# Intra-chunk attention levels of an HGRN2 layer on TensorE: 64-wide instead of 32-wide blocks, and two visits a turn instead of three

## What is computed

```python
def step(S, inp):
    qc, kc, vc, lc = inp
    b = jnp.cumsum(lc, axis=2)
    o = jnp.einsum('bhtd,bhde->bhte', qc * jnp.exp(b), S)
    diff = b[:, :, :, None, :] - b[:, :, None, :, :]
    decay = jnp.where(causal, jnp.exp(jnp.where(causal, diff, 0.0)), 0.0)
    a = jnp.einsum('bhtd,bhsd,bhtsd->bhts', qc, kc, decay)
    o = o + jnp.einsum('bhts,bhse->bhte', a, vc)
    ...
```

## Time and profile before

| what | value |
| --- | --- |
| median of 3 runs | 975.35 us (973.83 to 975.71) |
| the profiled execution: its own time | 975.35 us |
| its span | 973.5 us |
| TensorE busy | 953.5 us, 98% |
| VectorE, ScalarE, GpSimd busy | 620.1, 398.8, 395.4 us |
| mean granted clock of TensorE | 0.994 of full |

### The profile page before, as it was taken

The page is one execution under the profiler, slowest core; times in us unless marked ns, Lnnn a source line. Parts: engine busy times, 40 slices in busy tenths (PEclk is TensorE's granted clock), DMA queues, the critical chain, the costliest instruction groups (busy, mean ns, idle before and its releaser), DMA issues.

```text
span 973.5 us, 23670 instructions
## 1 busy us (share of the span) xinstructions
PE 953.5 (98%) x9958; PEld 902.2 (93%) x9958; DVE 620.1 (64%) x1223; ACT 398.8 (41%) x794; POOL 395.4 (41%) x295
## 2 busy tenths in 40 slices
PE   6999999999999999999999999999999999999996
PEld 6999999999999999899999999999998788788896
DVE  6467667667676766738932226467667867877635
ACT  7522324242424234325432233432227757865423
POOL 2265445454545444512244441442105534445343
PEclk9999999999999999999999999999999989999999
DMA  9521222313131313333233323321113223333104
GB/s 364 185 67 54 83 70 67 91 45 113 46 91 45 91 46 113 110 113 100 81 131 131 131 87 114 88 88 44 44 45 94 68 65 94 98 102 84 37 30 145
DMA packets 52921, 89.96 MB, mean 92 GB/s; under 512 B 15720, under 2 KB 34760, under 8 KB 52688
## 3 DMA queue, kind: packets, MB, share of 16 engines
q1 hardware_dynamic: 52528, 88.10, 28.2%
q10 hardware_dynamic: 288, 0.35, 0.1%
HBM read 70.80 MB, written 17.64 MB: 91 GB/s over the span
## 4 chain that ended last, share of the span: by engine, by line
PE 95%; DVE 2%; ACT 1%; issue 1%; DMA 0%; SPq 0%; DVEq 0%; ACTq 0%
PE G L1732 67%; PE G L2039 8%; PE R L1801 3%; PE R L1732 2%; PE R L1970 2%; PE R L1984 2%; PE R L1823 1%; PE R L1812 1%; PE R L1826 1%; PE R L2014 1%; PE R L2004 1%; PE R L1763 1%; PE R L1776 1%; DVE SP L1570 0%; PE R L1832 0%
## 5 line engine op out<-in xcount | busy, mean ns | idle before, releaser
L1732 PE MATMUL G<-XH,WH 128*128 128x344 f32 x1160 | 375.4, 326 | 7.5 <-ACT XH L963 7.5
L1732 PE MATMUL G<-XL,WH 128*128 128x344 f32 x1160 | 370.7, 322 | 1.5 <-DVE XL L1350 0.8
L1732 PE MATMUL G<-XH,WL 128*128 128x344 f32 x744 | 235.5, 320 | 0.0
L1732 PEld LDWEIGHTS G<-XH,WH 128*128 128x128 f32 x1160 | 218.7, 189 | 14.9 <-issue 12.3
L1732 PEld LDWEIGHTS G<-XL,WH 128*128 128x128 f32 x1160 | 218.3, 189 | 4.6 <-issue 3.2
L711 POOL TENSOR_TENSOR WL<-WR,WH 128x1024 fp32r<-128x1024 f32 x40 | 103.0, 2574 | 183.2 <-ACT WH L864 183.2
L1732 PEld LDWEIGHTS G<-XH,WL 128*128 128x128 f32 x744 | 139.7, 188 | 0.0
L1732 PE MATMUL G<-XL,WL 128*128 128x344 f32 x416 | 133.4, 321 | 0.0
L797 POOL TENSOR_TENSOR SP<-SP,small 128x1024 f32<-128x1024 f32 (+1 forms) x32 | 57.2, 1789 | 116.1 <-DVE small L1581 116.1
L745 POOL TENSOR_TENSOR K<-K,FP 128x512 f32<-128x512 f32 x48 | 66.6, 1388 | 73.7 <-PE R L1801 52.5
L864 ACT ACTIVATE WH<-WR 128x1024 fp32r<-128x1024 f32 x58 | 61.2, 1055 | 78.5 <-PE G L1732 52.6
(11 more groups left out here) (279 smaller groups left out, 1747.5 us busy)
## 6 DMA issues: line engine op xcount, KB each, us to landing
WR<-w SPq DMA_DIRECT2D x58, 512.0 KB, 3.9
A<-x SPq DMA_DIRECT2D x8, 516.0 KB, 7.2
FG<-head_scales SPq DMA_DIRECT2D x8, 516.0 KB, 3.6
RESO<-x SPq DMA_DIRECT2D x8, 516.0 KB, 4.5
h_spill<-H SPq DMA_DIRECT2D x8, 516.0 KB, 3.0
gate_spill<-EV SPq DMA_DIRECT2D x24, 172.0 KB, 2.1
RES<-h_spill SPq DMA_DIRECT2D x24, 172.0 KB, 2.5
SS<-states SPq DMA_DIRECT2D x8, 512.0 KB, 5.9
```

Of the source, the lines that this page charges most:

```text
L1732: return nc.tensor.matmul(U[unit_bank(NU * n + i)][:, 0:TU], w[:, n % 3, k, :], x[:, seg(i)], start=(k == 0 and p == 0), stop=(k == KT - 1 ...
```

## The change

For heads 0 to 6, levels 1 to 3 are done in slot 2, and levels 4 to 6 in slot 5; before, level 1 and half of level 2 in slot 2, the rest of 2 and level 3 in slot 4, levels 4 to 6 in slot 6. The transposes of the values move from slot 4 to slot 5, behind the levels, and their copies with them. VectorE's updates 3, 4 and 5 move from slot 4 to 2 (in front of the masked copies of levels 1 to 3), update 6 from 6 to 5. GpSimd's updates 3, 4 and 5 move from slot 4 to the start of slot 3, ahead of `prepare`; update 6 from 6 to 5; `decode_parts` from 3 to 4. ScalarE's copies of keys for levels 4 and 5 move from slot 5 to the start of slot 3, ahead of `prepare` and of the gates. For all eight heads the piece of levels 1 to 4 is 64 tokens wide instead of 32.

```diff
-    return {2: ((1, 0, NC), (2, 0, NC // 2)), 4: ((2, NC // 2, NC), (3, 0, NC)), 6: ((4, 0, NC), (5, 0, NC), (6, 0, NC))}
+    return {2: ((1, 0, NC), (2, 0, NC), (3, 0, NC)), 5: ((4, 0, NC), (5, 0, NC), (6, 0, NC))}
 def turned_values(r):
-    return 2 if r == HEADS - 1 else 4
+    return 2 if r == HEADS - 1 else 5
...
             for slot in range(9):
+                if slot == 3 and 0 <= r < HEADS - 1:
+                    for l in (3, 4, 5):
+                        update_k(r, l)
                 if slot % 3 == 0:
                     prepare(3 * it + slot // 3 + 2)
...
-                if slot == 3:
+                if slot == 4:
                     decode_parts(r)
-                for l in {0: (0, 1, 2), 4: (3, 4, 5), 6: (6,)}.get(slot, ()):
+                for l in {0: (0, 1, 2), 5: (6,)}.get(slot, ()):
                     update_k(r, l)
...
+                if slot == 3 and r >= 0:
+                    for l in copied_levels(r)[2:4]:
+                        copy_keys(r, l)
                 if slot % 3 == 0 and (it or slot):
                     prepare(3 * it + slot // 3 + 2)
...
-                if slot == 5 and r >= 0:
-                    for l in copied_levels(r)[2:4]:
-                        copy_keys(r, l)
...
-                    if r < HEADS - 1 and slot == 4:
+                    if r < HEADS - 1 and slot == 2:
                         for l in (3, 4, 5):
                             update_q(r, l)
-                    if r < HEADS - 1 and slot == 6:
+                    if r < HEADS - 1 and slot == 5:
                         update_q(r, 6)
...
-            w = max(32, 2 * h)
+            w = max(64, 2 * h)
```

## The result

The changed kernel takes 983.12 us (median of 6 runs, 981.6 to 984.54), beside 975.34 us for the kernel before (6 runs): a ratio of 1.0081, with a 95% interval of 1.0065 to 1.0097. It is slower, by 7.8 us; that is less than one per cent, but the interval is clear of 1. The profiled execution took 984.04 us, 0.9 us above the median, for a span of 982.0 us, 8.5 us longer than the span before; the mean granted clock is 0.994 in both.

A forecast was written before the change was run, and what follows sets the result against it. TensorE, busy 98% of the span, was taken to bound the kernel by the sum of its steps. Seven heads' +6.6 us and head 7's +1.4 make +8.0 on 975.35: 983.4 us, range 980 to 988.

The forecast's parts named there:

- step 1: Matmuls of levels 1 to 4, heads 0 to 6: rounds last as long as their weight loads, net +1.20 us a head.
- the load's own slope: Lower bound for levels 1 to 4: rounds cost 0.83 ns a column, mean 47 ns, -2.7 us, 980.7 us.
- step 2: TensorE's seams around the level visits, heads 0 to 6: 1.35 us before, 1.09 after, net -0.26 us a head.
- Per head: Heads 0 to 6 on TensorE: matmuls and seams together +0.94 us each, +6.6 us for seven heads.
- step 3: Head 7's four levels: matmuls from 2.14 to 3.30 us, seams from 0.28 to 0.55, together +1.4 us.
- The others and their cover: VectorE, GpSimd, ScalarE and SP: moved work comes later but stays covered; VectorE's 7.4 us piece has 6.6 us cover.
- all at nothing: Other engines' moved and delayed work, including weight loads, was priced at no added time.
- rival (c): New stall from VectorE's 7.4 us piece or later copies: 1 us a head gives 990 us; chance 0.07.
- The sum: Whole kernel: 6.6 + 1.4 = +8.0 us on 975.35 us, giving 983.4 us.

The follow-up runs named there:

- run 3: Changed kernel with levels 1 to 4 loading only 34 weight columns, same number of matmuls in two column tiles: 973.97 us, ratio 0.9986.
- run 4: Changed kernel with only 16 of 32 moving columns in each matmul of levels 1 to 4, weights unchanged: 983.04 us, ratio 1.0085.
- Run 1: Kernel before with pieces of levels 1 to 4 widened to 64 tokens, its three visits kept: 985.53 us, ratio 1.0111.
- run 2: Changed kernel with pieces of 32 tokens again, so only the two merged visits are left of the change: 980.58 us, ratio 1.006.
- run 8: Kernel with two visits and 32-token pieces, plus some 170 satisfied waits a turn between unit matmuls in slots 4 and 7: 1037.08 us, ratio 1.0632.
- run 7: Kernel with two visits and 32-token pieces, plus 32 small matmuls (128 instructions) at the program's start: 985.09 us, ratio 1.0109.
- run 9: Changed kernel with only level 3 of heads 0 to 6 in 64-token pieces, levels 1, 2 and 4 and head 7 at 32: 980.03 us, ratio 1.0039.
- run 10: Changed kernel with 32-token pieces in head 7 and level 4, and head 4's last-turn scaling moved behind the chunk states: 979.76 us, ratio 1.0044.

## Why the prediction was right

**Rounds and weight loads (step 1): right.** Taken were 56.5, 55, 52 and 46 ns; the rows after give 57, 54, 50 and 45, a mean of 51.4 against 52.4. Runs 3 and 4 separate the two operands: the columns of weights set the round, those of the moving operand don't. Whether it is the load itself isn't shown. The line from 34 ns at 32 columns to 58 at 64 was the better choice than the load's own slope with nothing beside it, which gives 47. The rule of the Trainium skill (TensorE: Matmul & The Clock Gate, section LDWEIGHTS) agrees with how the loads grow, 111 to 137 ns from 32 to 64 columns, but a round measured 3 to 5 ns more than the 52, 50, 47 and 40 it would give. The rule of the Trainium skill (TensorEngine Tiling (Array Packing), section Instruction Overhead), about 60 cycles for each matmul however few its columns, is contradicted: the records went from 8.7 to 28.4 ns apart with half as many of them, and run 3's are 16.8 ns apart.

**Seams (step 2): right in size.** (The terms as written add up to 1.37 before and 1.10 after, where 1.35 and 1.09 stand; it changes nothing.) The two visits were put at 3.0 and 2.7 us from unit to unit and measured 2.99 and 2.74. Between levels 1 and 2 the starts are 0.93 us apart, where 16 rounds make 0.90; between 2 and 3 0.88, as 16 rounds do. Run 1 less the change shows what the merged visit gives: 2.4 us, 0.34 a head with an uncertainty of the runs of about 0.2, against 0.26.

**Per head.** Forecast +0.94; measured 5.9/7 = 0.85 by the starts of level 1. In the two visits of head 1 themselves it is 6.25 - 4 x 0.16 = 5.61 after (108.64 to 111.89, 122.90 to 125.90, the natural steps taken off) against 5.71 - 6 x 0.16 = 4.75 before, +0.86. That head had the long seam between levels 1 and 2, 0.12 where most have 0.05, so in most heads it is some 0.93, as forecast, and 0.06 us or so is given back elsewhere in a turn; where wasn't found.

**Head 7 (step 3, its levels): right.** +1.4 forecast, +1.41 measured.

**The others and their cover: half right.** In seven heads nobody waited, as forecast. VectorE's timeline after, head 1, which answers to the earlier trace rows:

```profile
111.75 0.69 DVE L1288 TENSOR_TENSOR QU<-QU,FP 128x512 f32<-128x512 f32 x1 [1.18 <-PE R L1804]
...
116.28 3.00 DVE L1215 COPY_PREDICATED AT<-lmask,R 126x512 f32<-126x512 uint8 x3
119.19 0.91 DVE L1209 TENSOR_TENSOR RAWQ<-G,RB 128x344 f32<-128x344 f32 x2
```

The piece runs from 111.75 to 119.2, 7.4 us as summed. It begins 1.35 us later than the 110.4 that was put down, since the whole program was 0.43 us late by then and head 0 had added its 0.85; TensorE's second visit was late by as much, and the cover stayed as forecast. In head 7 the term "all at nothing" failed: 0.88 us, by VectorE's scaling in the last turn. This is rival (c) in kind, once and not per head, and by a way that the prediction didn't look at: not a wait for what the change makes late, but two engines' operations that now start in the other order.

**The sum.** Forecast +8.0; in the two profiled executions +8.5, made of 5.9 for seven heads (6.6 forecast), 1.4 for head 7 (1.4), 0.9 for the last turn (0) and 0.4 that was there ahead of the first level, less a tenth or two. The medians are 7.8 apart. Two errors, of -0.7 and +0.9, cancel: that 983.4 came within 0.3 us of the median is luck in part, while the sizes of the rounds and seams are not.

**What the prediction didn't know.** It gave the merged visit 0.26 us a head and the wide pieces a price, as if the two could be had apart. In these runs they couldn't. From one level 1 to the next, run 2's turns without a stall do take 45.83 to 45.93 us, a mean of 45.87, where those before took 46.10 to 46.20, a mean of 46.15: 0.28 less, as forecast. But with narrow pieces TensorE stops in other turns for its own instructions. The kernel before, with level 2 in two halves, and the change, with half as many records, both keep every burst of the levels under 256 instructions; this is a use of either that the sum doesn't show. Nothing in the trace of before hinted at it but the size of the queue's packets.

## What to carry to other kernels

Where small float32 matmuls go to several column tiles, price a round by the columns of its stationary operand: wider pieces in fewer tiles bring fewer instructions and take longer, unless the columns stay as few as they were. Count the instructions of a burst as well as its time: before work of 8 ns a record is gathered in one place, see whether it exceeds the block in which the engine's program arrives, and spread it with long matmuls between if it does. Filling up with satisfied waits is no way out (run 8). And when something off the critical path shifts, look at which of two engines' large elementwise operations starts first, not only at whether each has time.

## What the runs showed of the hardware

- TensorE's instructions come in packets of 16 KB, 256 instructions. A burst of 384 in 1.7 us stopped it for 1.75 to 2.3 us in about every third head, and the heads that stopped changed when 128 instructions were put in at the start (runs 2 and 7). Each stall ended 2.3 to 2.9 us after a packet began to move. Bursts of 192, 224 and 256 never stopped in the levels in these runs; one of 320 did once in seven heads (run 9).
- Behind one such stall (run 2, head 1) the granted clock was 0.50 for about 3 us, from 2.4 to 1.2 GHz, and a unit's step 0.29 us instead of 0.16. So it was behind the stall of head 6 in run 7, of 1.84 us. Behind the stall of head 4 in run 2, also of 2.32 us, and behind the others of runs 2, 7 and 9 it stayed at 1.00; what decides between them is open.
- Waits of TensorE that are long satisfied aren't free between matmuls: with 170 more instructions of them a turn, in front of 48 matmuls, steps of 0.16 us became 0.43 to 0.54 in one unit and 0.33 to 0.43 in the other, all but the first six and twelve steps of these units (run 8).
- In two column tiles a round lasts 34 ns at 34 columns of weights, 45 at 48, 57 at 62; with 16 moving columns as with 32 (runs 3 and 4).
- VectorE's scaling of 128x1032 took 1.29 us where it began ahead of GpSimd's subtraction of 128x1024 and 3.48 us where it began 0.02 us behind it; GpSimd's took 3.12 to 3.42 and 2.40. Three slots earlier, 0.25 us behind, it took 3.24 in both kernels; in run 10, 1.45 us behind, 2.03. In each of these it ended 1.1 us after GpSimd's. What the two share wasn't tried apart.
